# Differential attention with two query blocks under way, and attention steps placed by VectorE's times

## The reference, cut to what matters

```
s_f = q_f @ k_f.T * scale - slope * distance      # f = 0, 1, masked above the diagonal
a   = softmax(s_0) - lam * softmax(s_1)
o   = a @ v                                        # v is 256 wide
o   = rmsnorm(o) * g_head * (1 - lambda_init)
```

## Time and profile before

| what | value |
|---|---|
| median of three runs | 3925.5 us (3919.31 to 3929.22) |
| the profiled execution's own time | 3924.53 us |
| its span, first to last instruction | 3922.7 us |
| mean granted TensorE clock | 0.976 |
| TensorE busy | 3692.0 us (94%) |
| VectorE busy | 1805.7 us (46%) |
| ScalarE busy | 1325.9 us (34%) |
| GpSimd busy | 295.7 us (8%) |

### The profile page before, as it was taken

The page is one execution under the profiler, slowest core; times in us unless marked ns, Lnnn a source line. Parts: engine busy times, 40 slices in busy tenths (PEclk is TensorE's granted clock), DMA queues, the critical chain, the costliest instruction groups (busy, mean ns, idle before and its releaser), DMA issues.

```text
span 3922.7 us, 53647 instructions
## 1 busy us (share of the span) xinstructions
PE 3692.0 (94%) x23179; PEld 3000.0 (76%) x23179; DVE 1805.7 (46%) x2513; ACT 1325.9 (34%) x2053; POOL 295.7 (8%) x328
## 2 busy tenths in 40 slices
PE   7989999988899998999998999998999999599998
PEld 6777888867678886888886778886877777478887
DVE  4334434444443444543343344344656656445443
ACT  4444322333332232232234443224332333343222
POOL 1001100100010011110010011012000000000001
PEclk9999999989999999999999999998999999799999
DMA  6212323311122332332331123233222212332332
GB/s 208 65 49 70 97 91 102 96 55 52 61 92 91 100 100 75 97 94 90 103 96 54 52 78 97 92 97 98 78 58 62 79 53 67 125 111 89 104 94 69
DMA packets 333231, 337.44 MB, mean 86 GB/s; under 512 B 11857, under 2 KB 323779, under 8 KB 332484
## 3 DMA queue, kind: packets, MB, share of 16 engines
q1 hardware_dynamic: 332578, 333.89, 27.6%
q10 hardware_dynamic: 418, 0.12, 0.0%
HBM read 319.29 MB, written 14.68 MB: 85 GB/s over the span
## 4 chain that ended last, share of the span: by engine, by line
PE 86%; DVE 5%; ACT 5%; issue 2%; DMA 1%; ACTq 0%; POOL 0%; SPq 0%; POOLq 0%; DVEq 0%
PE P L99 85%; ACT sA L114 2%; ACT hi L113 1%; PE P L102 1%; DVE lo L117 1%; DVE x L117 0%; DVE mp L122 0%; DVE ds L125 0%; DVE rw_S L117 0%; DMA scr<-held_dram 0%; ACTq L154 0%; ACT scr L114 0%; DMA vg<-held_v_dram 0%; DVE st L134 0%; DMA rows<-in_shift_b_dram 0%
## 5 line engine op out<-in xcount | busy, mean ns | idle before, releaser
L117 DVE TENSOR_TENSOR lo<-raw,hi 128x1024 fp32r<-128x1024 f32 (+2 forms) x617 | 738.7, 1198 | 1177.6 <-ACT hi L113 1176.9
L99 PE MATMUL P<-aH,lo 128*128 128x512 f32 x2840 | 1142.6, 402 | 28.6 <-DVE q L125 11.4
L99 PE MATMUL P<-aH,hi 128*128 128x512 f32 x2840 | 1114.6, 392 | 0.0
L99 PE MATMUL P<-aL,hi 128*128 128x512 f32 x2840 | 1114.4, 392 | 0.0
L113 ACT ACTIVATE hi<-raw 128x1024 fp32r<-128x1024 f32 (+2 forms) x617 | 610.5, 991 | 1033.3 <-PE P L99 1027.2
L99 PEld LDWEIGHTS P<-aH,lo 128*128 128x128 f32 x2840 | 538.7, 190 | 160.8 <-issue 21.2
L99 PEld LDWEIGHTS P<-aH,hi 128*128 128x128 f32 x2840 | 538.0, 189 | 115.3
L99 PEld LDWEIGHTS P<-aL,hi 128*128 128x128 f32 x2840 | 539.3, 190 | 111.6 <-issue 5.4
L99 PE MATMUL P<-bH,lo 128*128 128x512 f32 x1088 | 426.1, 392 | 16.0 <-DVE bL L117 16.0
L99 PE MATMUL P<-bH,hi 128*128 128x512 f32 x1088 | 424.9, 391 | 0.0
L99 PE MATMUL P<-bL,hi 128*128 128x512 f32 x1088 | 424.9, 391 | 0.0
(11 more groups left out here) (284 smaller groups left out, 3884.5 us busy)
## 6 DMA issues: line engine op xcount, KB each, us to landing
raw<-in_w_ffn_in_dram SPq DMA_DIRECT2D x176, 512.0 KB, 3.5
raw<-in_w_in_dram SPq DMA_DIRECT2D x163, 512.0 KB, 3.8
raw<-in_w_ffn_out_dram SPq DMA_DIRECT2D x96, 384.0 KB, 3.0
raw<-in_w_ffn_dram SPq DMA_DIRECT2D x36, 512.0 KB, 3.6
raw<-in_w_o_dram SPq DMA_DIRECT2D x26, 512.0 KB, 3.5
raw<-in_w_ffn_dram SPq DMA_DIRECT2D x32, 384.0 KB, 3.1
raw<-in_w_mem_kv_dram SPq DMA_DIRECT2D x16, 512.0 KB, 4.3
raw<-in_w_ffn_out_dram SPq DMA_DIRECT2D x16, 512.0 KB, 3.4
```

The costliest lines, as they stand in the source:

```text
L99: return self.e.matmul(out, l, r, start=start, stop=stop, skip_group_check=skip) if self.e else Nothing()
L117: return self.e.tensor_tensor(out, a, b, op) if self.e else Nothing()
```

## The change

1. `diff_scores` builds slope * distance minus the product, so the sign is turned: a row minimum takes the place of the maximum, and ScalarE's exponential has scale -1.0 and the minimum as its bias. The negation is gone.
2. The two reciprocals become one on two columns; the product with lambda and the scaling become one tensor_scalar with two operands.
3. Blocks q = 2, 3 use `ds`, blocks q = 0, 1 a second buffer `dx`. `dx0` lies over the constant K_SCAN, which a transfer loads again in layer 2; the scan of the second network waits for it.
4. The order of a head is scores 3, scores 1, turn 3, scores 2, turn 1, scores 0, turn 2, turn 0 in place of 0, 1, 2, 3 each with its turn.
5. VectorE's part of both kinds of turn becomes a step of its own, `diff_probs` and `mem_probs`, with no TensorE part, planned by VectorE's time (`dve`, `gap`); the fixed 9.0 and 8.5 us are gone.
6. The q job of a group g >= 2 needs only the scores of the heads of group g-2 ("scored"); the v job needs what the q job needed.

```diff
-        for q in range(4):
-            out += [Step("diff_scores", l, h, q, 0, u, pe=0.22 * (q + 1), lat=0.2, needs=[("qkv", l, h)] if q == 0 else []),
-                    Step("diff_scores", l, h, q, 1, u, pe=0.22 * (q + 1), lat=9.0),
-                    Step("diff_turn", l, h, q, u, pe=0.11 * (q + 1), lat=1.2)]
-        out += [Step("diff_values", l, h, u, pe=4.4, lat=3.5, needs=[("mem", l)] if h >= 2 else [], gives=[("free", l, h)]),
+        def scores(q):
+            w = 0.27 * (q + 1)
+            return [Step("diff_scores", l, h, q, 0, u, pe=0.22 * (q + 1), dve=w + 0.4, needs=[("qkv", l, h)] if q == 3 else []),
+                    Step("diff_scores", l, h, q, 1, u, pe=0.22 * (q + 1), far=0.0, dve=w + 0.4, gap=0.6 + 0.11 * (q + 1),
+                         gives=[("exp", l, h, q)] + ([("scored", l, h)] if q == 0 else []))]
+        def turn(q):
+            return [Step("diff_probs", l, h, q, u, far=0.0, wait=0.0, dve=0.7 + 0.2 * (q + 1), needs=[("exp", l, h, q)], gives=[("probs", l, h, q)]),
+                    Step("diff_turn", l, h, q, u, pe=0.11 * (q + 1), far=1.2, needs=[("probs", l, h, q)], gives=[("turned", l, h, q)])]
+        out += scores(3) + scores(1) + turn(3) + scores(2) + turn(1) + scores(0) + turn(2) + turn(0)
+        out += [Step("diff_values", l, h, u, pe=4.4, lat=2.0, needs=[("turned", l, h, 0)] + ([("mem", l)] if h >= 2 else []), gives=[("free", l, h)]),
...
-        out += [Step("mem_scores", l, n, pe=0.9, lat=8.5, needs=[("mq", l)] if n == 0 else []),
-                Step("mem_turn", l, n, pe=0.9, lat=2.0),
+        out += [Step("mem_scores", l, n, pe=0.9, far=0.0, dve=1.6, gap=3.2, gives=[("mem_exp", l, n)], needs=[("mq", l)] if n == 0 else []),
+                Step("mem_probs", l, n, far=0.0, wait=0.0, dve=1.8, needs=[("mem_exp", l, n)], gives=[("mem_probs", l, n)]),
+                Step("mem_turn", l, n, pe=0.9, lat=2.0, needs=[("mem_probs", l, n)]),
...
-        jobs.append(Job(("q", l, g), W, l, 256 * g, 256, a, "q", norm=2 * l, needs=free, arg=g))
+        jobs.append(Job(("q", l, g), W, l, 256 * g, 256, a, "q", norm=2 * l, needs=scored, arg=g))
...
-        jobs.append(Job(("v", l, g), W, l, 2 * D + 256 * g, 256, a, "v", form="N", norm=2 * l, arg=g, gives=[("qkv", l, g)]))
+        jobs.append(Job(("v", l, g), W, l, 2 * D + 256 * g, 256, a, "v", form="N", norm=2 * l, needs=free, arg=g, gives=[("qkv", l, g)]))
...
-        e.stt(s, c[:, K_DIST + 512 - w:K_DIST + 512], -slope, P[:, 2 + 3 * u + f, 0:w], ALU.mult, ALU.add
+        e.stt(s, c[:, K_DIST + 512 - w:K_DIST + 512], slope, P[:, 2 + 3 * u + f, 0:w], ALU.mult, ALU.subtract
-        e.rmax(mx, s).then_inc(*S.dve_attn.up())
-        e.wait_ge(*S.dve_attn.now())
-        e.ts(nm, mx, -1.0, None, ALU.mult).then_inc(*S.dve_attn.up(("max", l, h, q, f)))
+        e.rmin(least, s).then_inc(*S.dve_attn.up(("least", l, h, q, f)))
...
-    def diff_turn(l, h, q, u):
+    def diff_probs(l, h, q, u):
...
-        e.recip(inv0, total0)
-        e.recip(inv1, total1).then_inc(*S.dve_attn.up())
+        e.recip(inv, total).then_inc(*S.dve_attn.up())
-        e.tt(inv1, inv1, st[:, 4:5], ALU.mult).then_inc(*S.dve_attn.up())
-        e.ts(s1, s1, inv1, None, ALU.mult).then_inc(*S.dve_attn.up())
+        e.ts(s1, s1, inv[:, 1:2], st[:, 4:5], ALU.mult, ALU.mult).then_inc(*S.dve_attn.up())
...
+        e.wait_ge(*S.scan_in.at(0))
         e.scan(A["cs"], c[:, K_SCAN:K_SCAN + 512], A["lwd"]).then_inc(*mine.up((p, "cs")))
...
+        if h == 0 and l == KINDS.index(1) + 1:
+            e.wait_ge(*S.attended.at(("turn", l - 1, 2, 0)))
+            e.dma(m["c"][:, K_SCAN:K_SCAN + 512], d["const"][:, K_SCAN:K_SCAN + 512]).then_inc(*S.scan_in.up(0, by=16))
...
+    at("dx0", [2, 256], off=cc + 4 * K_SCAN)
+    at("dx1", [2, 256], off=ex + 8192)
```

More of the change, by code:

```diff
@@ L131, in recip, with rmin @@
         return self.e.reciprocal(out, in_) if self.e else Nothing()
+    def rmin(self, out, in_):
+        return self.e.tensor_reduce(out, in_, AX.X, ALU.min) if self.e else Nothing()
     def rmax(self, out, in_):
@@ L263, in stick_steps @@
     for h in heads:
-        out += [Step("stick_scores", l, h, u, pe=2.2, lat=7.0, needs=[("qkv", l, h // 2)]),
+        out += [Step("stick_scores", l, h, u, pe=2.2, lat=7.0, needs=[("qkv", l, h // 2)], far=0.0, gives=[("scored", l, h)]),
                 Step("stick_split", l, h, u, lat=3.5), Step("stick_sums", l, h, u, pe=2.5, lat=4.0),
@@ L313, in qkv_jobs @@
     for g in range(4):
-        free = []
-        if g >= 2:
-            free = [("head", l, 2 * g - 4), ("head", l, 2 * g - 3)] if KINDS[l] == 0 else [("free", l, g - 2)]
-        jobs.append(Job(("q", l, g), W, l, 256 * g, 256, a, "q", norm=2 * l, needs=free, arg=g))
+        scored = free = []
+        if g >= 2 and KINDS[l] == 0:
+            scored, free = [[(x, l, h) for h in (2 * g - 4, 2 * g - 3)] for x in ("scored", "head")]
+        elif g >= 2:
+            scored, free = [[(x, l, g - 2)] for x in ("scored", "free")]
+        jobs.append(Job(("q", l, g), W, l, 256 * g, 256, a, "q", norm=2 * l, needs=scored, arg=g))
         jobs.append(Job(("k", l, g), W, l, D + 256 * g, 256, a, "k", norm=2 * l, arg=g))
-        jobs.append(Job(("v", l, g), W, l, 2 * D + 256 * g, 256, a, "v", form="N", norm=2 * l, arg=g, gives=[("qkv", l, g)]))
+        jobs.append(Job(("v", l, g), W, l, 2 * D + 256 * g, 256, a, "v", form="N", norm=2 * l, needs=free, arg=g, gives=[("qkv", l, g)]))
     return jobs
@@ L563, in vec, with scores, diff_cols @@
         return self.v[:, 128 + 8 * j + p:129 + 8 * j + p]
+    def scores(self, u, q):
+        return self.m["ds"][u] if q > 1 else self.m["dx"][u]
+    def diff_cols(self, u, q):
+        k = 24 + 12 * u + 6 * (q < 2)
+        return [self.st[:, k + 2 * j:k + 2 * j + 2] for j in range(3)]
     def operand(self, src):
@@ L783, in diff_turn @@
         for j in range(q + 1):
-            t = e.tp(P[:, b, 128 * j:128 * j + 128], m["ds"][u][:, 0, 128 * j:128 * j + 128], ident)
+            t = e.tp(P[:, b, 128 * j:128 * j + 128], K.scores(u, q)[:, 0, 128 * j:128 * j + 128], ident)
         t.then_inc(*S.attended.up(("turn", l, h, q)))
@@ L1308, in stick_values @@
         e.act(m["mixH"][:, h, :], bank(2 + 3 * u), ACT.Copy).then_inc(*S.act_value.up((l, h)))
-    def diff_cols(u, f):
-        k = 24 + 8 * u + 4 * f
-        return [st[:, k + j:k + j + 1] for j in range(4)]
     def diff_scores(l, h, q, f, u):
[L1315 to L1318, removed]
+        s = K.scores(u, q)[:, f, 0:128 * (q + 1)]
+        least, total, inv = K.diff_cols(u, q)
+        e.wait_ge(*S.dve_attn.at(("least", l, h, q, f)))
+        e.act(s, s, ACT.Exp, -1.0, least[:, f:f + 1], total[:, f:f + 1]).then_inc(*S.act_attn.up(("exp", l, h, q, f)))
     def diff_turn(l, h, q, u):
@@ L1322, in diff_turn @@
         e.wait_ge(*S.attended.at(("turn", l, h, q)))
-        if q == 0 and h >= 2:
+        if q == 3 and h >= 2:
             e.wait_ge(*S.dve_value.at((l, 2 * (h - 2) + 1)))
@@ L1715, in stick_values @@
         e.tt(m["mixL"][:, h, :], bank(2 + 3 * u), m["mixH"][:, h, :].bitcast(F32), ALU.subtract).then_inc(*S.dve_value.up((l, h)))
-    def diff_cols(u, f):
-        k = 24 + 8 * u + 4 * f
-        return [st[:, k + j:k + j + 1] for j in range(4)]
     def diff_scores(l, h, q, f, u):
         w, slope = 128 * (q + 1), 2.0 ** (-8.0 * (h + 1) / 4)
-        s = m["ds"][u][:, f, 0:w]
-        mx, nm, total, inv = diff_cols(u, f)
+        s, least = K.scores(u, q)[:, f, 0:w], K.diff_cols(u, q)[0][:, f:f + 1]
@@ L1733, in diff_turn @@
-    def diff_turn(l, h, q, u):
+        e.rmin(least, s).then_inc(*S.dve_attn.up(("least", l, h, q, f)))
+    def diff_probs(l, h, q, u):
         w = 128 * (q + 1)
-        s0, s1 = m["ds"][u][:, 0, 0:w], m["ds"][u][:, 1, 0:w]
-        (_, _, total0, inv0), (_, _, total1, inv1) = diff_cols(u, 0), diff_cols(u, 1)
-        e.wait_ge(*S.act_attn.at(("exp", l, h, q, 0)))
-        e.recip(inv0, total0)
-        e.wait_ge(*S.act_attn.at(("exp", l, h, q, 1)))
-        e.recip(inv1, total1).then_inc(*S.dve_attn.up())
+        s0, s1 = K.scores(u, q)[:, 0, 0:w], K.scores(u, q)[:, 1, 0:w]
+        least, total, inv = K.diff_cols(u, q)
+        for f in range(2):
+            e.wait_ge(*S.act_attn.at(("exp", l, h, q, f)))
+        e.recip(inv, total).then_inc(*S.dve_attn.up())
@@ L1741, in diff_turn @@
         e.wait_ge(*S.dve_attn.now())
         e.wait_ge(*S.evict.at("lambda set"))
-        e.tt(inv1, inv1, st[:, 4:5], ALU.mult).then_inc(*S.dve_attn.up())
+        e.ts(s1, s1, inv[:, 1:2], st[:, 4:5], ALU.mult, ALU.mult).then_inc(*S.dve_attn.up())
         e.wait_ge(*S.dve_attn.now())
-        e.ts(s1, s1, inv1, None, ALU.mult).then_inc(*S.dve_attn.up())
-        e.wait_ge(*S.dve_attn.now())
-        e.stt(s0, s0, inv0, s1, ALU.mult, ALU.add).then_inc(*S.dve_attn.up(("probs", l, h, q)))
+        e.stt(s0, s0, inv[:, 0:1], s1, ALU.mult, ALU.add).then_inc(*S.dve_attn.up(("probs", l, h, q)))
```

11 lines of the change are left out of this document (6 added, 5 removed).

## The result

The changed kernel takes 3823.9 us (median of four runs, 3817.1 to 3826.6) where the kernel before takes 3924.8 (four runs): ratio 0.9741, 95% interval 0.9723 to 0.9759. The forecast was 3854, with a range of 3828 to 3895. The direction was right; the gain was 101 us in place of 72, and the time lies 4 us under the range.

A forecast was written before the change was run, and what follows sets the result against it. TensorE, busy 94% of the span, was taken as the bound, so only its waits and low-clock time counted. Terms 26 + 22 + 12 - 4 + 16 = 72 us off 3924.5 gave 3854 after rounding, range 3828 to 3895.

The forecast's parts named there:

- The cause: Transposes in layer 1 and memory attention wait 61.5 us together because VectorE's part is queued too late in its list.
- turns of layer 1: Layer 1's transposes, waiting 31.9 us for `ds`: VectorE's part as its own step gains 26 us (15 to 32).
- turns of memory attention: Transposes in four layers, waiting 29.6 us for `mp`: the same step gains 22 us (13 to 30).
- q jobs: `sA`, `mixL`: Layers 0 and 3: projections needing only scores fill TensorE's waits, 12 us gained (0 to 15).
- new bank wait: Layer 1: scores 1's second product waits about 1 us per head for a PSUM bank, 4 us lost.
- clock: Low-clock stretches in the attention layers: 16 us come back of up to 27.7, bounds 5 and 24.
- six stretches in ten go: Attention layers: six in ten low-clock stretches vanish with the long waits, giving 16 us.
- rival A: All stages: waits go but the clock keeps falling behind short waits, 16 us less gain, 3870; chance 0.22.
- 0.4 us a turn, 6 us: Layer 1: what stays of the transposes' waits, for ScalarE conversions in front of the exponential.
- the `recip` of a turn beginning within 1 us of the row sum: Sign of being right: VectorE starts normalising within 1 us of ScalarE's finished row sum.
- the ends don't come together, so I draw them in: Whole-kernel range: summed bounds 3825 and 3905 were narrowed to 3828 and 3895.
- The hole from 982.71 to 1006.82: Layer 1 before the output projection: 24.1 us without projection work, taken as filled because heads get 27 us shorter.
- The smaller operations: VectorE's negations, reciprocals and products: 9.9 us less work, counted 0 because it lies beside TensorE's work.

The follow-up runs named there:

- e5: The changed kernel with VectorE's part of both kinds of turn carried out at the transposes again, planned times and both buffers kept: 3881.0 us.
- e9: The kernel before with only VectorE's part of both turns as a step of its own, placed by planned times: 3846.2 us.
- e7: The changed kernel with every transpose of a turn planned 1.6 us earlier behind VectorE's part: 3846.1 us.
- e6: The changed kernel with memory attention planned and placed as before in all four layers: 3850.9 us.
- e4: The changed kernel with one buffer, the old order of query blocks and no reload of K_SCAN: 3809.0 us.
- i1: The changed kernel with stick-breaking attention's softplus as a VectorE step of its own, placed by a planned ScalarE time: 3816.6 us.
- e2: The kernel before with only the early q jobs, needing just the scores, and the v jobs' needs changed to match: 3905.8 us.

## Why the prediction was right in kind and short in size

*The cause.* "It is queued at the place of the transposes, behind work that TensorE itself has just released" was right, shown by both e5 (57 us lost by undoing it) and e9 (77 us won by the place with its planned times alone). Most of what the forecast missed lies in layer 1: it was to be 38 us shorter and is 58.6.

*The terms.* Forecast and measured, in the profiled executions:

| term | forecast | measured |
|---|---|---|
| turns of layer 1 | 26 | 31.9 (31.9 to 0) |
| turns of memory attention | 22 | 22.9 (29.6 to 6.7) |
| q jobs: `sA`, `mixL` | 12 | 13.4 (15.2 to 1.8) |
| new bank wait | -4 | -2.5 (4 x 0.6) |
| other waits (`q`, `x`, `dT`) | none | 7.8 (11.4 to 7.2; 21.5 to 20.0; 3.6 to 1.5) |
| clock | 16 | 23.5 |
| sum | 72 | 97 of 99.5 |

The clock (7.5 us short) and the waits counted at nothing (7.8) were sized worst, then the turns of layer 1 (5.9). The low-clock stretches of these stages, before with five more that the prediction didn't list, and after:

```profile
sum 23.89, PE 19.64 PEld 15.45 DVE 22.44 ACT 13.10 POOL 3.13; mean PE 3.93 PEld 3.09 DVE 4.49 ACT 2.62 POOL 0.63
```

```profile
sum 34.13, PE 28.09 PEld 22.63 DVE 27.74 ACT 17.11 POOL 3.95; mean PE 4.01 PEld 3.23 DVE 3.96 ACT 2.44 POOL 0.56
```

TensorE was busy 37.81 + 17.58 + 19.64 = 75.0 us at 1.2 GHz before and 28.1 after; half of the difference is 23.5 us. The step that failed first is the discount on this term, "six stretches in ten go". All fourteen stretches of rows 10 and 11 went. The trace of before could have shown it: each of them stands at a wait of 1.80 to 5.51 us for `ds`, `mp`, `sA` or `q`, and the change took all of these waits away. The five unlisted ones stand at waits of 3.33 to 6.30 us for `x` and `q` that stayed, and stayed with them; two new ones stand at the `mp` waits of 3.37 us in layers 0 and 3. A wait of such a length doesn't always bring a fall: the one of 3.56 us at 1508.05 had none before.

The prediction held against rival A that the four falls in rows 11 were all that layers 0, 2 and 3 add. That was a misreading, there are eight. The rule cited from the Trainium skill ("TensorE: Matmul & The Clock Gate", "A second HAM failure mode: psum-queue depth-cycling"), by which micro-idles suffice, is not borne out in layer 1 of e7: 11.9 us in short waits there, and a clock of 0.99. It isn't ruled out for the whole kernel. In the second network of the changed kernel the clock fell to 1.2 GHz behind no longer waits than these:

```profile
3090.59 1.10 PE L99 MATMUL P<-rw_r,c 128*128 128x512 f32 x2 [1.21 <-DVE rw_r L128]
3093.40 2.07 PE L99 MATMUL P<-rw_r,c 128*128 128x512 f32 x2 [1.72 <-ACT rw_r L113]
```

```profile
3092.77:3099.59 6.82, 6.19 (x11) 3.52 (x12) 0.69 (x1) 1.21 (x3) 0.00 (x0) 0.50 0.00 0
```

The second failure is "0.4 us a turn, 6 us" for what stays of the turns in layer 1. It charged a lateness that the plan's own spacing covers: VectorE's part ended 3.6 us ahead of the transposes above, and with 1.6 us less of it (e7) all sixteen turns together waited 2.0 us for VectorE. For the same reason the sign to look for, "the `recip` of a turn beginning within 1 us of the row sum", did not come about: the row sum was there at 799.59 us and the reciprocal began at 801.55, and nobody waited. The third is that waits for `q`, `x` and `dT` were counted at nothing. They stand queued in the same lists. The waits for `q` fell with memory attention's edit: they are 7.2 us in e9 and 11.4 in e6. All six terms came out above the forecast, and "the ends don't come together, so I draw them in" took 3825 out of the range when the terms did come together. Even that end lies 1 us above the time measured.

*What held.* The hole from 982.71 to 1006.82 is gone, for the reason given, that heads are short. From its first product of scores to its first product with the values the first head takes 29.3 us where it took 63.6. With one buffer (e4) that is 34.1, and the hole is gone too, so it is the planned times that did this and not the second block under way. Memory attention's term was met (22 and 22.9), but not as told: in place of half a microsecond at each turn, two waits of 3.37 us are left, and that the sums agree is partly luck. The new wait of a `k,q` product is there, 0.61 us where 1 was said. The smaller operations were put at 0 "once the turns don't wait"; alone they gave 5.6 us, as the turns still wait there. With two operands the scaling takes longer than with one, within the 0.2 us allowed (mean of one in ns):

```profile
L122 DVE TENSOR_SCALAR ds<-ds,st 128x512 f32<-128x512 f32 x4 | 2.2, 546 | 0.1
```

It was 486 ns. At the three smaller widths it went from 420 to 480, from 353 to 413 and from 287 to 346 ns, so the second operand costs about 60 ns whatever the width. The reload of K_SCAN landed beside other transfers, and layer 2, where it is, has no idle time:

```profile
c<-const_dram SPq DMA_DIRECT2D x1, 256.0 KB, 3.9
```

The `mp` wait of 3.4 us that is left in each of layers 0 and 3 fits what the prediction named, ScalarE's time being in no plan: with a planned time for ScalarE (i1) both waits go, to 0.4 us.

## What to carry to other kernels

In a list that engines walk in order, the place of an engine's part decides more than its length (77 us against 5.6 here): give each engine's part of a step its own place, when its inputs are there and not when its reader comes. Before sizing a clock term, list all low-clock stretches with the wait that each stands at. Where the change takes all of these waits away, count the work at half clock at its full size. When several terms hang on one cause, add their ends when the range is drawn.

## What the runs showed of the hardware that was not expected

The window behind layer 3's attention, with the same 12691 matmuls in every variant, is between 1556 and 1572 us long in the fourteen traces. That is up to 15 us that no edit makes in its own stage, as much as one of the smaller edits here, and it is why stages are compared by window and not by the whole time. Most of it is the clock: TensorE's work at 1.2 GHz in this window goes from 31.8 us (e4) to 59.2 (e2), and half of that difference is 13.7 us, where the two windows differ by 13.6. Why the clock falls more often in one variant than in another there, with the same work, stays open.
